# The end of the second block's mixer: which engine scales what, and in what order

## What is computed

```
q, k, v, q_idx, k_idx, w_idx, qk_m, v_m, o_m, i_pre, f_pre = split(rmsnorm(x) @ w_in)
att  = sparse attention: 8 heads of 64, each query keeps the 64 best keys by index score
qk_m = silu(causal_conv(qk_m));  q_m, k_m = split(qk_m)          # conv over 4 tokens
# mLSTM, 4 heads of 128, two chunks of 128 tokens
C    = sum over chunk 0 of exp(a - a_max) k v^T                   # the state, and its key sum n
num  = w_inter * (q C) + ((q k^T) * w_intra) v
h    = num / max(|den|, exp(-m_t))
h_m  = rmsnorm(h, m_norm) * sigmoid(o_m)
x    = x + concat(att, h_m) @ w_out
```

## Time and profile before

| | us |
|---|---|
| Median of 3 runs | 2267.3 (2265.55 to 2268.49) |
| The profiled execution's own time | 2264.18 |
| Its span | 2262.4 |
| TensorE busy | 2165.1 (96% of the span) |
| VectorE busy | 1506.6 (67%) |
| ScalarE busy | 1073.5 (47%) |
| GpSimd busy | 563.0 (25%), all but 10.2 of it in the first block |

### The profile page before, as it was taken

The page is one execution under the profiler, slowest core; times in us unless marked ns, Lnnn a source line. Parts: engine busy times, 40 slices in busy tenths (PEclk is TensorE's granted clock), DMA queues, the critical chain, the costliest instruction groups (busy, mean ns, idle before and its releaser), DMA issues.

```text
span 2262.4 us, 39808 instructions
## 1 busy us (share of the span) xinstructions
PE 2165.1 (96%) x17241; PEld 2075.5 (92%) x17241; DVE 1506.6 (67%) x1866; ACT 1073.5 (47%) x1414; POOL 563.0 (25%) x274
## 2 busy tenths in 40 slices
PE   7999999999999999999999999989999999989999
PEld 7988889899988888989999999879999999869999
DVE  6877676787677776667666556776556556686554
ACT  2666563433456647444345335454445344545333
POOL 0873314899248250375000000000000000000000
PEclk7999999999999999999999999999999999989999
DMA  9752335677566224566555555325555555425553
GB/s 292 243 172 88 113 112 188 226 253 241 192 188 205 93 68 145 165 218 204 172 186 172 184 186 170 109 76 185 186 187 169 186 187 168 131 75 161 180 184 128
DMA packets 332856, 383.93 MB, mean 170 GB/s; under 512 B 12551, under 2 KB 315402, under 8 KB 332554
## 3 DMA queue, kind: packets, MB, share of 16 engines
q1 hardware_dynamic: 332234, 381.23, 52.4%
q10 hardware_dynamic: 448, 0.16, 0.0%
HBM read 380.32 MB, written 1.05 MB: 169 GB/s over the span
## 4 chain that ended last, share of the span: by engine, by line
PE 76%; DVE 11%; ACT 8%; issue 3%; SPq 1%; DMA 0%; ACTq 0%; DVEq 0%
PE bank L734 16%; PE bank L736 16%; PE bank L735 16%; DVE weights_low L1363 5%; PE bank L963 5%; PE bank L964 5%; PE bank L965 5%; ACT weights_high L2071 4%; DVE arena L1465 1%; PE bank L748 1%; SPq L666 1%; PE bank L1000 1%; PE bank L1160 1%; PE bank L1145 1%; PE bank L763 1%
## 5 line engine op out<-in xcount | busy, mean ns | idle before, releaser
L1363 DVE TENSOR_TENSOR weights_low<-ring,weights_high 128x2048 fp32r<-128x2048 f32 x302 | 752.1, 2490 | 444.9 <-ACT weights_high L2071 444.5
L734 PE MATMUL bank<-h_high,weights_high 128*128 128x256 f32 x3296 | 943.9, 286 | 23.7 <-DVE weights_low L1363 14.6
L735 PE MATMUL bank<-h_low,weights_high 128*128 128x256 f32 x3296 | 927.0, 281 | 0.0
L736 PE MATMUL bank<-h_high,weights_low 128*128 128x256 f32 x3296 | 926.6, 281 | 0.0
L2071 ACT ACTIVATE weights_high<-ring 128x2048 fp32r<-128x2048 f32 x302 | 578.1, 1914 | 708.1 <-PE bank L736 546.7
L734 PEld LDWEIGHTS bank<-h_high,weights_high 128*128 128x128 f32 x3296 | 621.6, 189 | 41.9 <-DVE weights_low L1363 22.0
L735 PEld LDWEIGHTS bank<-h_low,weights_high 128*128 128x128 f32 x3296 | 622.5, 189 | 3.9 <-issue 3.8
L736 PEld LDWEIGHTS bank<-h_high,weights_low 128*128 128x128 f32 x3296 | 622.4, 189 | 0.0
L963 PE MATMUL bank<-hidden_high,weights_high 128*128 128x256 f32 x1056 | 299.1, 283 | 1.3 <-DVE hidden_low L1605 0.8
L964 PE MATMUL bank<-hidden_low,weights_high 128*128 128x256 f32 x1056 | 298.4, 283 | 0.0
L965 PE MATMUL bank<-hidden_high,weights_low 128*128 128x256 f32 x1056 | 298.4, 283 | 0.0
(11 more groups left out here) (422 smaller groups left out, 2838.3 us busy)
## 6 DMA issues: line engine op xcount, KB each, us to landing
ring<-in_w_in SPq DMA_DIRECT2D x80, 1024.0 KB, 5.3
ring<-in_w_up SPq DMA_DIRECT2D x44, 1024.0 KB, 5.2
ring<-in_ffn_w_gate SPq DMA_DIRECT2D x44, 1024.0 KB, 5.4
ring<-in_ffn_w_up SPq DMA_DIRECT2D x44, 1024.0 KB, 5.3
ring<-in_ffn_w_down SPq DMA_DIRECT2D x44, 1024.0 KB, 5.0
side<-in_w_ada SPq DMA_DIRECT2D x42, 1024.0 KB, 7.7
ring<-in_w_down SPq DMA_DIRECT2D x22, 1024.0 KB, 5.0
ring<-in_w_dn_out SPq DMA_DIRECT2D x8, 1024.0 KB, 5.2
```

The source lines that it names most:

```text
L734: mm(o[:, m, :], a_, high[:, t, :], start=(t == 0), stop=False)
L735: mm(o[:, m, :], a_, low[:, t, :], start=False, stop=False)
L736: last = mm(o[:, m, :], b_, high[:, t, :], start=False, stop=(t == KT - 1))
L1363: v.tensor_tensor(low, wide(q), high.bitcast(F32), ALU.subtract).then_inc(chunk_split, 1)
```

## The change

Seven edits, all in the second block's mixer, in both layers:

1. `hW` is made earlier on ScalarE, ahead of the mLSTM's exponentials, and GpSimd multiplies it by `rinv` (two instructions, 128x1024). So `conv_scale` goes for `qk` 2 and 3 (their taps read PSUM) and `om_scale` goes.
2. GpSimd multiplies the queries with their decay.
3. ScalarE scales the keys (four Copy activations, with `1/sqrt(128)` moved into the exponential's bias).
4. The state products stand ahead of `om` 1, into other banks; head 3's scores stand between the two halves of `om` 1.
5. The gate is `0.5 * (1 + tanh(x/2))`: Tanh and an Identity on ScalarE for each of two chunks, one ahead of the keys and one between the two lots of exponentials; the 0.5 goes into the instruction that puts the rms factor on h.
6. Table loads: one ahead of the gate, one after the exponentials of lot 1; those for the sigmoids and for the next norm go. The rounding of output chunk 0 comes before all of this. The rms factor comes after all of lot 0's copies and pairs.
7. Transposes of the probabilities go to the two `L` banks in place of `B[3]` and `B[4]`; the transposes of h stand inside lot 1; lot 0 is normalised after lot 1's masking; three pairs get their low part before the gate; the output projection takes its tiles in the order 0 to 7.

```diff
@@ TensorE
-                linear_uncut(("om", l, 1))
-                scores(0, one_group, 3, 4)
-                scores(1, one_group, 0, 3)
                 pe.wait_ge(m_kx, l + 1)
-                pe.wait_ge(in_copied, INC["vm", l, 1])
+                pe.wait_ge(in_copied, INC["om", l, 0])
                 for j in range(4):
-                    last = mm(B[3 if j < 2 else 4][:, (j % 2) * T:(j % 2) * T + 129], mKX[:, j, :], vaug[:, 0, j, 0:129], start=True, stop=True)
+                    o = B[5][:, j * P4:j * P4 + 129] if j < 3 else L[R["om", l, 0] % 2][:, 0:129]
+                    last = mm(o, mKX[:, j, :], vaug[:, 0, j, 0:129], start=True, stop=True)
                 last.then_inc(m_state, 1)
-                scores(1, one_group, 3, 4)
+                linear_uncut(("om", l, 1), lambda: scores(0, one_group, 3, 4))
+                scores(1, one_group)
+                pe.wait_ge(m_scored, l + 1)
+                pe.wait_ge(m_query, l + 1)
                 pe.wait_ge(m_ca, l + 1)
...
-                pe.wait_ge(m_read, l + 1)
+                pe.wait_ge(in_copied, INC["om", l, 1])
                 weigh_sparse(0)
...
+                weigh_sparse(1, turn_state)
                 for i in range(4):
-                    linear3_tiles(("out", l, i), merged_high, merged_low, (0, 1, 4, 5, 6, 7, 2, 3), pairs if i == 0 else None, (m_split, l + 1))
+                    linear3_tiles(("out", l, i), merged_high, merged_low, range(KT), pairs if i == 0 else None, (m_split, l + 1))
@@ VectorE
                 for i in range(4):
-                    conv_scale(("qk", l, i), 24 + 4 * l + i)
+                    if i < 2:
+                        conv_scale(("qk", l, i), 24 + 4 * l + i)
...
-                     v.tensor_tensor(mQD, mQD, qkm[:, 0:4, P:T], ALU.mult))
-                dve.wait_ge(m_keys, l + 1)
-                v.scalar_tensor_tensor(out=mKX, in0=f4(B[5][:, :]), scalar=float(P) ** -0.5, in1=bcast(ca, P), op0=ALU.mult, op1=ALU.mult).then_inc(m_kx, 1)
...
-                om_scale(0)
-                masked(sparse_store, 1, IM, None, lambda: normalised(sparse_store, 0, None))
+                masked(sparse_store, 1, IM, None)
+                normalised(sparse_store, 0, None)
...
-                om_scale(1)
@@ ScalarE
+                for t in range(KT):
+                    ins = a_(hW[:, t, :], x[:, t, :], ACT.Identity, bias=0.0, scale=vcol[:, vd, 8 + t:9 + t])
+                ins.then_inc(h_plain, 1)
                 values_out(0)
...
+                split(SI["out", l, 0] + 1)
+                nc.scalar.preload_act_table_set("exp_and_others")
+
+                def open_out(i):
+                    act.wait_ge(chunk_multiplied, M["om", l, i] + 1)
+                    gate = gab[:, 2 * i:2 * i + 2, :]
+                    a_(gate, LV[R["om", l, i] % 2], ACT.Tanh, scale=0.5).then_inc(in_copied, 1)
+                    act.wait_ge(in_copied, INC["om", l, i])
+                    a_(gate, gate, ACT.Identity, bias=col(COL_ONE), scale=1.0).then_inc(gates_opened, 1)
+
+                open_out(0)
+                act.wait_ge(m_keys, l + 1)
+                ca = sm(23, 4)
+                ins = [a_(mKX[:, j, :], B[5][:, j * P:(j + 1) * P], ACT.Copy, scale=ca[:, j:j + 1]) for j in range(4)]
...
+                exps(sparse_store, 0, False)
+                open_out(1)
+                exps(sparse_store, 1, False)
                 nc.scalar.preload_act_table_set("natural_log_exp_and_others")
@@ GpSimd, for each layer, after the rope squares
+                pool.wait_ge(norm_factor, 4 + 3 * l + 2)
+                pool.wait_ge(h_plain, l + 1)
+                ins = [g_.tensor_tensor(hW[:, t:t + 4, :], hW[:, t:t + 4, :], over(rinv[:, :], 4), ALU.mult) for t in (0, 4)]
+                then(ins[0])
+                ins[1].then_inc(h_whole, 1)
+                pool.wait_ge(m_expd, l + 1)
+                pool.wait_ge(silu_done, 24 + 4 * l + 2)
+                g_.tensor_tensor(mQD, mQD, qkm[:, 0:4, P:T], ALU.mult).then_inc(m_query, 1)
```

More of the change, by code:

```diff
@@ L737, in linear3, with linear_uncut @@
                 last.then_inc(chunk_multiplied, 1)
-            def linear_uncut(key):
+            def linear_uncut(key, between=None):
                 q = Q[key]
@@ L746, in linear_uncut @@
                 for m in range(2):
+                    if m and between is not None:
+                        between()
                     for t in range(KT):
@@ L921, in attention_gated, with weigh_sparse @@
                     cnt["lot"] += 1
-            def weigh_sparse(lot):
+            def weigh_sparse(lot, between=None):
                 values = lambda tt: vtok[:, tt, 0:64]
@@ L931, in weigh_sparse @@
                         turn(sparse_store, cnt["lot"] % 2, h4 + 1)
+                    if h4 == 2 and between is not None:
+                        between()
                     weigh(4 * lot + h4, n0 + h4, sparse_store, values)
@@ L1453, in conv @@
             def conv(key, n, cols):
-                src = XV[:, n % 2, :].rearrange("p (m t) -> p m t", m=2) if key[0] == "qk" else PLACE[key]
+                src = XV[:, n % 2, :].rearrange("p (m t) -> p m t", m=2) if key[0] == "qk" and key[2] < 2 else PLACE[key]
                 dve.wait_ge(tap_done, n + 1)
@@ L1512, in lower, with masked @@
                 lowered[0] += 1
-            def masked(store, lot, mask, sink, third=None):
+            def masked(store, lot, mask, sink):
                 gl = lots[0] + lot
@@ L1521, in masked @@
                 for h4 in range(4):
-                    if h4 == 3 and third is not None:
-                        third()
                     n = scored[0]
@@ L2012, in _ @@
                 lower(sparse_store)
-                dve.wait_ge(in_copied, INC["om", l, 1])
+                lower(sparse_store)
+                dve.wait_ge(gates_opened, 2 * l + 2)
                 dve.wait_ge(m_turned, l + 1)
@@ L2103, in first_tap @@
             def first_tap(key, n, tap, bias=None):
-                if key[0] == "qk":
-                    act.wait_ge(conv_scaled, 4 * key[1] + key[2] + 1)
+                if key[0] == "qk" and key[2] < 2:
+                    act.wait_ge(conv_scaled, 2 * key[1] + key[2] + 1)
                     ps = XV[:, n % 2, :].rearrange("p (m t) -> p m t", m=2)
@@ L2432, in _ @@
                         split(SI["qk", l, 1] + 1)
-                        for t in range(KT):
-                            ins = a_(hW[:, t, :], x[:, t, :], ACT.Identity, bias=0.0, scale=vcol[:, vd, 8 + t:9 + t])
-                        ins.then_inc(h_whole, 1)
                     if i < 4:
@@ new lines, in _ @@
+                exps(sparse_store, 0, False)
+                open_out(1)
+                exps(sparse_store, 1, False)
+                nc.scalar.preload_act_table_set("natural_log_exp_and_others")
+                for lot in range(2):
+                    for _ in range(2):
+                        copy_turned(sparse_store)
+                        copy_turned(sparse_store)
+                        round_pair(sparse_store)
+                    if lot == 0:
+                        act.wait_ge(m_w, l + 1)
+                        rsqrt(sm(27, 8), sm(27, 8), 1.0 / P, 0.0, m_factor)
```

83 lines of the change are left out of this document (31 added, 52 removed).

## The result

| | us |
|---|---|
| Before, median of 14 runs | 2266.19 (2264.3 to 2269.89) |
| After, median of 14 runs | 2270.06 (2267.4 to 2271.82) |
| Ratio | 1.0018, 95% interval 1.001 to 1.0025 |
| The profiled execution's own time | 2268.91 |
| Its span | 2267.1 |

The changed kernel is 0.18% slower, 3.9 us. Forecast was 8.2 us faster, 2255.0 to 2264.5; the result lies outside that range and on the other side.

What follows compares the result with a forecast made beforehand. One chain, from best keys through exponentials and copies to the tile needing h_m, was taken to bound it. Gains of 4.5 and 6.7 us, 11.2, less 3 for low clock: 8.2 faster, 2259.1 us, range 2255.0 to 2264.5.

Steps and rivals of the forecast that it cites:

- VectorE's masks, `om` 0, keys, state, half of `om` 1, exponentials: Chain up to the first copy: masks at 1470.8, keys 1469.1, first exponential 1477.2 (was 1480.00), copies 1489.0 (was 1493.89).
- The end: From rms factor to the tile needing h_m, TensorE meanwhile on lot 1 and transposes: tile at 1503.8, 3.8 us earlier.
- The clock: TensorE's clock falls to its lower level over lot 0 in each layer, costing 1.5 us per layer, 3 us.
- The 0.7 us for four finished tiles: Output chunk 0 has four tiles done, not two, when h_m comes; at 0.35 us each this gains 0.7 us.
- the sum before the clock: Both layers' gains on the chain, 4.5 us in the first and 6.7 in the second: 11.2 us faster.
- Rival 1: No low clock spell over lot 0: 11.2 us faster, 2256.1 us; chance 0.20.
- Rival 2: Second low clock spell, over output chunk 0, some 2.5 us per layer: 3.2 us faster, 2264.1; chance 0.16.
- Rival 3: ScalarE's two table loads per layer have a drain ahead, 2.7 us per layer: 2.8 us faster, 2264.5; chance 0.08.
- Rival 4: Low clock holds from lot 0 to the end of output chunk 0: 9.8 us slower, 2277; chance 0.06.
- GpSimd: VectorE's split for `qk` 0 slowed beside GpSimd's product: taken as 0 us per layer, bounds 0 to 0.9.

Runs made afterwards that it cites:

- the best version: The changed kernel with the rms factor early, value products in four banks instead of two, and spare matmuls: 2255.25 us against 2266.15, ratio 0.9952.
- three ways: The changed kernel with one edit each: rms factor earlier (2261.32 us), low part of head pair 0 earlier (2260.95 us), value products in four banks (2261.28 us).

## Why the prediction was wrong

- **VectorE's masks, `om` 0, keys, state, half of `om` 1, exponentials**: right, within 0.7 us at each point up to the first copy. 0.6 of it comes in at `qk` 0, whose products run that much later because VectorE's split for it is late beside GpSimd's product.
- **The end**: this step failed. It says that behind lot 0 "TensorE meanwhile does half of lot 1 and the transposes", while VectorE has factor, h, split and low parts. TensorE could not: its first weighing of lot 1 waits for one of those low parts. I had timed VectorE's list and TensorE's list side by side, and not asked whether an item of the second waits for an item of the first. The wait is in the code I had before me, the diff moves the factor past both roundings of lot 0, and before had some 0.2 us of room there. By the forecast's sum the gate starts at 1499.1 (1495.9 and 3.15), and it starts at 1507.58. Of these 8.5 us 3.1 come with h, which is done at 1498.96 and not 1495.9 (late copies and the low clock over lot 0), and 5.4 with lot 1. From there on the step holds (4.56 us to the tile, forecast 4.7).
- **The clock**: one low spell over lot 0 was right, its size of 1.5 us per layer too small. From the first copy to the rms factor it was 7.5 us and not 5.2, so 2.3, near the bound of 2.6 (5.1 us with spare matmuls, 1489.57 to 1494.68). The second spell, over lot 1, follows from the new wait: lot 1's first half takes 4.45 us (1501.63 to 1506.08), and 2.5 with full clock in the best version (1496.33 to 1498.80).
- **Size of the loss**: the wait and the low spell behind it cost 8.8 us (2270.06 to 2261.28). Without the wait the kernel is at 2261.3, 2260.9 or 2261.3 in three ways, inside the range and 4.9 to 6.4 us under the before beside it, where 8.2 was forecast; the second spell, over output chunk 0, is 3 us of that and was left to a rival. The 0.7 us for four finished tiles was right (5.33 to 4.62 from the tile to the first sum). With the clock full as well the best version gains 10.9 us, where the sum before the clock was 11.2. That the two are so close is in part luck: the best version has the factor early and four banks, while the change's own order with spare matmuls keeps the wait and gains only 4.6 (2266.15 to 2261.53). The terms up to the first copy and behind the gate stand, the end does not.
- **Rival 1** (no low spell) did not occur by itself; with spare matmuls, the factor early and four banks it is 2255.25, and it had said 2256.1 for the change as it was; with spare matmuls alone that is 2261.53.
- **Rival 2** (low clock over output chunk 0): not in the changed kernel (1.00 from 1508 on), but it appears as soon as the wait is gone, at 0.66 in the rows above. There it costs 1.5 us per layer, where the rival had 2.5.
- **Rival 3** (a drain ahead of table loads) is refuted where work is queued directly ahead of the load: the exponentials' last row starts at 1488.18 and takes 0.19, the load starts at 1488.38, 1.28 long, and the copy at 1489.67. The load ahead of the gate starts at 1465.71, 0.01 us behind the rounding. The Trainium skill (ScalarE: Activation LUTs, What ACT_TABLE_LOAD costs) gives 1.38 us of drain for each switch beside a load of 1.28; the trace agrees on the load and shows no drain here.
- **Rival 4** gave the right sign for a part of the right reason. It let the clock stay low through lot 1 by itself, and its own point against it, that the clock comes back, is what the trace shows (0.93 at 1496 to 1500) until the new wait takes it down again. No rival had a wait between TensorE and VectorE at lot 1, which is where the slower side was.
- **GpSimd**: taken as 0 per layer with bounds 0 to 0.9; it is 0.5 by the tiles. The cost lay at another place than argued: less on the split than on VectorE's rope products ahead of it, which take 6.1 us (1420.07 to 1426.19) where alone they take 1.8, so the split starts at 1426.22 and not at 1423.06.

## What to carry to other kernels

When an instruction is moved on one engine, list what stands behind its waiter on the other engine, and for each of these who waits for it; a small instruction can hold a PSUM bank through three others. Check a claim of "meanwhile" against every wait in the code of the work that is to go on. And where a wait and a low clock feed each other, price them together: here either repair alone, the wait or the clock, gave back 8.5 to 9.1 us, and both together 14.8 (by the chain 8.2 to 9.2, and 16.3). And look at the stretch behind the repair: with the wait gone, the clock fell over output chunk 0, where it had been full.

## What was not expected of the hardware

- Matmuls that compute nothing made the kernel faster by 8.5 us (2270.06 to 2261.53) and by 5.2 us (2261.32 to 2256.12), because the granted clock stayed at 1.00, 2.4 GHz, through stretches in which it had fallen to 0.50, 1.2 GHz. The same filling put where its own wait came late cost 5 us.
- VectorE's `scalar_tensor_tensor` with several SBUF inputs took 2.62 us beside GpSimd's product and 0.48 without it. The Trainium skill (SBUF — State Buffer, SBUF: two separate sides) says that a VectorE instruction with two SBUF inputs and a GpSimd instruction that reads SBUF lock each other out for a whole instruction; the trace agrees to within 0.2 us, since VectorE's last rope product, 0.48 us long by itself, ends 0.3 us behind GpSimd's second instruction (1426.19 and 1425.91).
- The low spell of a wait is not certain: behind waits of 2.1 and 2.6 to 3.3 us ahead of lot 0 it came in the changed kernel and in each experiment on it without spare matmuls; behind 2.66 us in the kernel before it did not come in the first layer. Nor is its start: the six transposes between the two waits took 1.32 us in the first layer of the changed kernel, so the clock fell behind 2.12 us alone, and 0.84 in the second, where it fell only within the next wait.
